# Own rows of a shared expert added by GpSimd in SBUF, and a last sum added by VectorE to TensorE's banks row tile by row tile

## What is computed

```python
def moe_ffn(x2d, ...):                      # x2d: 512 tokens x 1024
    ...                                     # 8 of 64 experts for each token, weights w
    # for each expert: its tokens gathered, swiglu(x[tok], w_exp_gu[e], w_exp_down[e]) * weight,
    # added to the tokens' rows: routed
    return routed + swiglu(x2d, w_sh_gu, w_sh_down)      # the shared expert sees every token

ff = moe_ffn(x, ...)
x = layer_norm_2(DEEPNORM_ALPHA * x + ff, ln3_g, ln3_b)   # DEEPNORM_ALPHA = 2 ** 0.25
```

## Time and profile before

| | |
|---|---|
| median of 3 runs | 2682.42 us (2681.78 to 2683.23) |
| the profiled execution | 2681.46 us, span 2679.5 us |
| TensorE (PE) busy | 2603.9 us, 97% |
| VectorE (DVE) busy | 1963.6 us, 73% |
| ScalarE (ACT) busy | 1410.6 us, 53% |
| GpSimd (POOL) busy | 278.8 us, 10% |
| moved by DMA | 435.49 MB, mean 163 GB/s |

### The profile page before, as it was taken

How to read it: one execution, slowest core, us unless ns; L and a number is a source line. 1 busy time by engine, 2 the same in 40 slices (tenths; PEclk the granted TensorE clock), 3 DMA queues, 4 the chain that set the end, 5 groups by cost and what they waited for, 6 DMA issues and landing times.

```text
span 2679.5 us, 34993 instructions
## 1 busy us (share of the span) xinstructions
PE 2603.9 (97%) x12355; PEld 2031.6 (76%) x12355; DVE 1963.6 (73%) x2844; ACT 1410.6 (53%) x2164; POOL 278.8 (10%) x242
## 2 busy tenths in 40 slices
PE   9999999999999999999999998999999999999996
PEld 7877878788887877888887775587667777777773
DVE  4788765777736985877736738456488999999996
ACT  4766652222324545322333233444456899898893
POOL 0000000000000000000000800000016622222210
PEclk9999999999999999999999999999999999999998
DMA  3222232222323123223233542323139999999997
GB/s 113 71 64 70 63 102 94 95 94 94 97 87 103 46 64 59 81 104 104 67 108 111 151 143 25 110 95 106 57 124 353 396 393 392 401 401 393 393 395 284
DMA packets 260215, 435.49 MB, mean 163 GB/s; under 512 B 45374, under 2 KB 199047, under 8 KB 235267
## 3 DMA queue, kind: packets, MB, share of 16 engines
q1 hardware_dynamic: 241795, 397.71, 42.0%
q0 software_dynamic: 18304, 36.26, 4.4%
HBM read 416.44 MB, written 42.62 MB: 171 GB/s over the span
## 4 chain that ended last, share of the span: by engine, by line
PE 85%; DVE 6%; DMA 3%; ACT 3%; issue 2%; DVEq 0%; SPq 0%; ACTq 0%; POOLq 0%
PE tp L1374 40%; PE tp L2081 4%; PE tp L2083 4%; PE tp L2082 4%; PE tp L1330 2%; PE tp L1480 2%; PE tp L1482 2%; PE tp L1481 2%; PE mp L2103 2%; PE mp L2105 2%; PE mp L2104 2%; PE tp L1421 2%; PE tp L2069 2%; PE tp L1879 1%; DMA uT<-in_w_exp_gu 1%
## 5 line engine op out<-in xcount | busy, mean ns | idle before, releaser
L1374 PE MATMUL tp<-sq_r,arena_r 128*128 128x512 f32 x1056 | 413.8, 392 | 5.8 <-DVE uT_r L2982 3.5
L1374 PE MATMUL tp<-uT_r,arena_r 128*128 128x512 f32 x1056 | 411.7, 390 | 0.0
L1374 PE MATMUL tp<-sq_r,wring_r 128*128 128x512 f32 x1056 | 411.7, 390 | 0.0
L1374 PEld LDWEIGHTS tp<-sq_r,arena_r 128*128 128x128 f32 x1056 | 198.6, 188 | 50.8 <-issue 7.3
L1374 PEld LDWEIGHTS tp<-sq_r,wring_r 128*128 128x128 f32 x1056 | 198.7, 188 | 41.7
L1374 PEld LDWEIGHTS tp<-uT_r,arena_r 128*128 128x128 f32 x1056 | 198.6, 188 | 41.3 <-issue 0.5
L2954 DVE TENSOR_TENSOR wring_r<-wring,arena_r 128x2048 fp32r<-128x2048 f32 x82 | 187.2, 2322 | 48.8 <-ACT arena_r L2244 48.5
L1374 PE MATMUL tp<-arena_r,wring_r 128*128 128x512 f32 x564 | 219.4, 389 | 0.0
L2492 ACT ACTIVATE arena<-arena 128x512 f32<-128x512 f32 x44 | 27.8, 633 | 288.1 <-DVE arena L3040 288.0
L2244 ACT ACTIVATE arena_r<-wring 128x2048 fp32r<-128x2048 f32 x82 | 152.2, 1902 | 39.4 <-DVE arena L3144 11.8
L3895 DVE TENSOR_TENSOR arena_r<-arena,arena_r 128x1024 fp32r<-128x1024 f32 x128 | 150.2, 1213 | 0.5 <-ACT arena_r L2839 0.5
(11 more groups left out here) (633 smaller groups left out, 6261.2 us busy)
## 6 DMA issues: line engine op xcount, KB each, us to landing
wring<-in_w_exp_gu SPq DMA_DIRECT2D x64, 1024.0 KB
arena<-in_w_exp_down SPq DMA_DIRECT2D x64, 1024.0 KB
uT<-in_w_exp_gu SPq DMA_DIRECT2D x32, 1024.0 KB
sq<-in_w_exp_gu SPq DMA_DIRECT2D x32, 1024.0 KB
wring<-in_f_up_w SPq DMA_DIRECT2D x22, 1024.0 KB, 5.0
wring<-in_f_up_w SPq DMA_DIRECT2D x44, 512.0 KB, 6.4
wring<-in_f_down_w SPq DMA_DIRECT2D x32, 448.0 KB, 5.3
wring<-in_a_in_proj SPq DMA_DIRECT2D x42, 256.0 KB, 2.7
```

Of the source, the lines that this page charges most:

```text
L1374: ins = nc.tensor.matmul(b[:], parts[wp][:, kk, m * P:(m + 1) * P], xparts[xp][:, kk, :], start=n_k == 0 and q == 0, stop=n_k == k - 1 and ...
```

## The change

The tokens' own rows leave TensorE. ScalarE now takes the banks of the shared expert alone, without a factor; GpSimd adds the own rows to each taken tile in SBUF (`own_row`, eight additions of 128x512), and signals `pool_tables`. The buffers are swapped: row tiles 0 and 1 go to `raw`, row tiles 2 and 3 to `ye`, and because `ye` is where the own rows of tiles 0 and 1 lie, ScalarE waits for two and then four additions before the fifth and the seventh tile. It waits for all eight before it rounds the first down weights. SyncE stores a row tile when its additions are done. GpSimd does four additions ahead of the gather of expert 2 and four ahead of that of expert 3. The index products and the one-hot tables move forward, the transposes of expert 1 go into the middle of expert 0's products, and VectorE's low parts are reordered. ALPHA comes in at the end, in VectorE's first addition.

At the end TensorE adds the tables 2, 5, 6 and 7 and no longer VectorE's sum. VectorE adds the tables 0, 1, 3 and 4, and when TensorE's banks of a row tile are complete it adds them to its own sum (`add_total`), one row tile ahead of the norm. ScalarE's sum of the rows now reads `fin` in SBUF and waits for `sums_ready`.

```diff
-        rest_halves = [[y[:, 512 * half:512 * half + 512] for half in range(2)] for y in ye]
-        rest_halves += [[raw[2 * k + half][:, PAD:PAD + 512] for half in range(2)] for k in range(2)]
+        rest_halves = [[raw[2 * k + half][:, PAD:PAD + 512] for half in range(2)] for k in range(2)]
+        rest_halves += [[y[:, 512 * half:512 * half + 512] for half in range(2)] for y in ye]
...
-                sp.wait_ge(tile_evac, RES_TILES - 8 + 2 * c + 2)
+                sp.wait_ge(pool_tables, 4 + 1 + 2 * c + 2)
                 rows = rest[c * P:(c + 1) * P, :]
-                if c < 2:
-                    sp.dma_start(rows, ye[c]).then_inc(first_ranks, 16)
+                if c >= 2:
+                    sp.dma_start(rows, ye[c - 2]).then_inc(first_ranks, 16)
                 else:
                     for half in range(2):
                         sp.dma_start(rows[:, 512 * half:512 * half + 512], rest_halves[c][half]).then_inc(first_ranks, 16)
...
+            def own_row(i):
+                pool.wait_ge(tile_evac, RES_TILES - 8 + i + 1)
+                natural = rest_halves[i // 2][i % 2].rearrange("p (q k) -> p q k", k=NK)
+                by_feature = row_tok[i // 2].rearrange("p (k q) -> p q k", k=NK)
+                G.tensor_tensor(natural, natural, by_feature[:, 64 * (i % 2):64 * (i % 2) + 64, :], ALU.add).then_inc(pool_tables, 1)
+
             put_entries(range(0, 6))
             m_gather(0, 0, 0, 1)
-            put_entries(range(6, 8))
+            put_entries(range(6, 7))
             m_gather(1, 1, 1, 2)
-            put_entries(range(8, 9))
+            for i in range(4):
+                own_row(i)
             m_gather(2, 0, 2, 3)
+            for i in range(4, 8):
+                own_row(i)
             m_gather(3, 1, 3, 4)
-            put_entries(range(9, 14))
...
-            def m_gu(n, b, q):
+            def m_gu(n, b, q, halfway=None):
                 wait(moe["xlo"], n + 1)
                 wait(moe["act"], n - 1)
                 hi, lo = [w[:, :].rearrange("p (k n) -> p k n", n=512) for w in (wgu_hi[b], wgu_lo[q])]
                 out = gu_bank(n, b)[0:CAP, :]
                 for k in range(NK):
+                    if k == 4 and halfway:
+                        halfway()
...
-            def own_row(i):
-                pe.wait_ge(tile_evac, RES_TILES - 8 + i - NBANK + 1)
-                by_feature = row_tok[i // 2].rearrange("p (k q) -> p q k", k=NK)
-                nc.tensor.matmul(down_bank(i), ident[:], by_feature[:, 64 * (i % 2):64 * (i % 2) + 64, :], start=True, stop=False)
-
...
-                nc.tensor.matmul(down_bank(i), sact_hi[k][:, rows], shd_hi[:, k, half], start=False, stop=False)
...
-            for i in range(NBANK):
-                own_row(i)
+            def first_half(i):
+                pe.wait_ge(tile_evac, RES_TILES - 8 + i - NBANK + 1)
+                shared_down(i, 0)
+
             pe.wait_ge(rt["weights"], 4 + NK + 4)
             for i in range(NBANK):
-                shared_down(i, 0)
-                if i in (0, 3):
-                    m_idx(i // 3, i // 3, i // 3)
+                first_half(i)
+                if i == 2:
+                    m_idx(0, 0, 0)
             pe.wait_ge(rt["weights"], 4 + NK + 5)
             for i in range(8):
                 if i >= NBANK:
-                    own_row(i)
-                    shared_down(i, 0)
+                    first_half(i)
                 shared_down(i, 1).then_inc(tile_done, 1)
                 tiles.inc()
-                if i in (1, 3):
-                    m_idx(2 + i // 2, 2 + i // 2, i // 2)
+                if i in (0, 2, 4):
+                    m_idx(1 + i // 2, 1 + i // 2, (1 + i // 2) % 2)
                 if i == 6:
                     m_turn(0, 0, 16)
             assert tiles.s == RES_TILES
-            m_turn(1, 1, 16)
-            m_gu(0, 0, 0)
+            m_gu(0, 0, 0, halfway=lambda: m_turn(1, 1, 16))
...
-
-            def add_sum(c):
-                pe.wait_ge(sums_ready, c + 1)
-                add_rank(c, rest_rows)
-
-            def add_last(c):
+            for c in range(TC):
+                pe.wait_ge(late_ranks[c], 16 * 2)
+                add_rank(c, rank_rows[5])
+            for c in range(TC):
                 pe.wait_ge(row_in[c], 16 * 3)
                 add_rank(c, rank_rows[6])
                 add_rank(c, rank_rows[7], last=True).then_inc(rank_sums, 1)
-
-            add_sum(0)
-            for c in range(1, TC):
-                add_sum(c)
-                add_last(c - 1)
-            add_last(TC - 1)
...
-            for c in range(TC):
-                for half in range(2):
-                    take(rest_halves[c][half], scale=ALPHA)
-                if c == 2:
-                    m_xhi(0, 0)
+            for i in range(7):
+                if i == 4:
+                    act.wait_ge(pool_tables, 4 + 1 + 2)
+                if i == 6:
+                    act.wait_ge(pool_tables, 4 + 1 + 4)
+                take(rest_halves[i // 2][i % 2])
+            m_xhi(0, 0)
+            take(rest_halves[3][1])
+            m_ghi(1, 1, 1, 32)
             m_xhi(1, 1)
-            m_ghi(1, 1, 1, 32)
             m_silu(0, 0)
+            act.wait_ge(pool_tables, 4 + 1 + 8)
             m_dhi(0, 0, 0, 16)
             m_acthi(0)
...
-                act.wait_ge(rank_sums, c + 1)
+                act.wait_ge(sums_ready, c + 1)
                 for half in range(2):
-                    ins = nc.scalar.activation(summed[half], total[c][half][:], ACT.Identity, accum_out=row_sums[:, c, half:half + 1])
+                    ins = nc.scalar.activation(unread[half], fin[c][:, 512 * half:512 * half + 512], ACT.Identity, accum_out=row_sums[:, c, half:half + 1])
...
+                if j == 1:
+                    m_onehot(0, 0, 0)
                 dve.wait_ge(rt["weights_hi"], 9 + j)
                 V.tensor_tensor(sact_lo[:, j, :], sact[:, j, :], sact_hi[j].bitcast(F32), ALU.subtract).then_inc(rt["weights"], 1)
...
-            m_onehot(0, 0, 0)
             m_onehot(1, 1, 1)
             assert nconv.s == CONVS
             m_conv(0, 0, 0, 0)
@@ -3929,14 +3932,14 @@
             m_onehot(3, 3, 1)
             m_glo(0, 0, 0, (0,))
             m_conv(2, 0, 2, 0)
+            m_onehot(4, 4, 0)
+            m_conv(3, 1, 3, -1)
             m_glo(0, 0, 0, (1,))
-            m_conv(3, 1, 3, -1)
-            m_onehot(4, 4, 0)
-            m_glo(0, 0, 0, (2,))
             m_xlo(0, 0)
-            m_glo(0, 0, 0, (3,))
+            m_glo(0, 0, 0, (2, 3))
+            m_glo(1, 1, 1, (0, 1))
             m_xlo(1, 1)
-            m_glo(1, 1, 1)
+            m_glo(1, 1, 1, (2, 3))
             m_act(0, 0, swt[0])
             m_dlo(0, 0, 0)
             m_actlo(0)
...
-                    add_rows(c, rank_rows[0])
+                    chain.inc()
+                    V.scalar_tensor_tensor(fin[c], fin[c], ALPHA, rank_rows[0][:, c, :], ALU.mult, ALU.add).then_inc(dve_chain, 1)
+                    added[c] = chain.v
...
-            def add_late(c):
+            for c in range(TC):
                 dve.wait_ge(late_ranks[c], 16 * 2)
-                for r in (4, 5):
-                    add_rows(c, rank_rows[r], last=r == 5)
+                add_rows(c, rank_rows[4])
+
+            def add_total(c):
+                dve.wait_ge(rank_sums, c + 1)
+                dve.wait_ge(dve_chain, added[c])
+                for half in range(2):
+                    s = slice(512 * half, 512 * half + 512)
+                    ins = V.tensor_tensor(fin[c][:, s], fin[c][:, s], total[c][half][:], ALU.add)
+                ins.then_inc(sums_ready, 1)
...
+                    ins = V.scalar_tensor_tensor(centred[half], fin[c][:, s], neg_mean[:, c:c + 1], g3[half], ALU.add, ALU.mult)
...
-                    V.scalar_tensor_tensor(fin[c][:, s], fin[c][:, s], inv_std[:, c:c + 1], b3[half], ALU.mult, ALU.add).then_inc(fin_ready, 1)
-
-            for c in range(TC):
-                add_late(c)
+                    V.scalar_tensor_tensor(fin[c][:, s], centred[half], inv_std[:, c:c + 1], b3[half], ALU.mult, ALU.add).then_inc(fin_ready, 1)
+
+            add_total(0)
             for c in range(TC):
                 mean_of(c)
                 link(centred_gain(c))
+                if c + 1 < TC:
+                    add_total(c + 1)
                 scale_of(c)
                 scaled_bias(c)
```

17 lines of the change are left out of this document (9 added, 8 removed).

## The result

| | before | after |
|---|---|---|
| median | 2682.33 us (9 runs, 2679.57 to 2683.23) | 2689.11 us (9 runs, 2685.6 to 2690.4) |
| the profiled execution | 2681.46 us, span 2679.5 | 2687.01 us, span 2685.3 |
| mean granted TensorE clock | 0.993 | 0.989 |

The ratio is 1.0022, 95% interval 1.0013 to 1.0030: a little slower, 6.8 us by the medians and 5.6 by the profiled executions. The forecast of 2682.7 was 6.4 us too low; the range held the time. A loss of this size is by the prediction's own bound of 0.2% just on the slower side. That the range held it is luck: its upper end, 2689.9, stood for additions of 2.2 us, and they took 1.5.

What follows compares the result with a forecast made beforehand. Weight transfers were taken to pace the experts, not TensorE. Start -2.3 us plus end +2.6 us gives +0.3 on 2682.42, so 2682.7 us; range 2675.8 to 2689.9 us.

Steps and rivals of the forecast that it cites:

- the prediction's own bound of 0.2%: Whole kernel: a change within 0.2% (5.4 us) is about what a measurement can't tell from none.
- The price of an addition: GpSimd's own-row additions at the start: 1.3 us each, plus 0.08 between two.
- the rival's reason: Start: strided additions cost nearly double, as on TensorE, delaying expert 3's weights; slower, up to 2689.9 us; chance 0.24.
- GpSimd and VectorE in turns: Start: last four additions alternate with VectorE's low parts through a shared SBUF port; the eighth ends at 2027.0.
- TensorE 4.2 us earlier at expert 0: Start: VectorE finishes expert 0's activation at 2032.1 instead of 2036.28, so TensorE is 4.2 us earlier.
- The six entries moved behind the last gather cost nothing: Start, GpSimd's queue: moved table entries cost nothing, since GpSimd is busy only 44.5 of 60 us.
- The experts' end depends on when the stream of weights begins: Experts: transfers set the pace; expert 3's weights issue at 2027.6 instead of 2029.94, ending the experts 2.3 us earlier.
- The prediction's own sign: Experts: if the forecast is right, ScalarE shows more and earlier waits for weights than before.
- The end: Last norm: 22.3 us instead of 19.7, 2.6 us longer, with a mean every 5.1 us.

Runs made afterwards that it cites:

- run 8: Changed kernel with one entry issued behind each of the eight additions instead of behind gather 3; 2693.06 us, ratio 1.0039.
- run 7: Changed kernel with two of its nine entries behind gather 3 put back ahead of the additions; 2685.09 us, ratio 1.0008.
- Run 11: Changed kernel with entries spread, the old end, and expert 3's weights issued ahead of the last two row tiles' stores; 2682.17 us, ratio 0.9997.
- run 12: Kernel before, with only expert 3's weights issued ahead of the last two row tiles' stores; 2680.66 us, ratio 0.9998.
- run 5: Changed kernel with five entries between gather 3 and gather 4 and two in each of steps 1 to 10; 2683.90 us, ratio 1.0006.
- run 3: Changed kernel with three entries instead of nine between gather 3 and gather 4, the others in later steps; 2684.95 us, ratio 1.0008.
- run 4: Changed kernel with twelve entries instead of nine between gather 3 and gather 4; 2696.24 us, ratio 1.0048.
- run 9: Changed kernel with two entries back ahead of the additions, none in step 0, two in each of steps 1 to 9; 2683.65 us, ratio 1.0006.

## Why the prediction was right or wrong

**The price of an addition: right.** 1.3 us plus 0.08 was forecast, 1.5 measured. That is 1.2 times the 1.27 us by size of an addition without the stride, so the stride may cost something on GpSimd, but not the doubling that was the rival's reason: the additions are not dear.

**GpSimd and VectorE in turns: wrong in form.** The step let VectorE do a low part between two additions. In fact it was held through each group of four (5.79 us for 0.15 us of work). For the additions that was good: they ended at 2025.14, not 2027.0. For VectorE it was dear, and still the transposes of expert 0's activation came only 1.7 us later than forecast (2.5 us earlier than before, from the mark, instead of 4.2). The Trainium skill, "SBUF — State Buffer", section "Who interferes with whom", says the first to issue holds the ports that both share and the other is blocked until it is done. By that rule one addition would have been the price of a wait; the trace shows a wait for four, and for one where an entry stood between (run 8).

**TensorE 4.2 us earlier at expert 0: sign right.** It was 2.5 us from the mark. The prediction took the half clock after pauses to cost up to 2.2 us at expert 1; the first pitch was 11.24 instead of 9.81, 1.4 us. Between the runs without a wait in it, it was anything from 0 to 2.5, the larger ones where TensorE had paused five times instead of three.

**"The six entries moved behind the last gather cost nothing": the step that failed.** The lists show two entries moved behind gather 3, seven becoming nine, not the six of the prediction nor the three of the section on the change. The prediction looked at GpSimd's busy share, 44.5 of 60 us, and not at who waits behind the entries. The queue is in order, and gather 4 stands behind them. Before, seven entries took 11.7 us (2031.40 to 2043.08) and gather 4 followed with 0.3 us between, so each entry more would put it off. By the 1.7 us an entry that these rows give with its pause, nine from 2027.40 would have let gather 4 go at 2042.8, no later than before. But after the change they took 2.3 each. An entry can take as little as 0.98 us. In the traces before and after, between 2000 and 2300 us, all 27 entries of 1.5 us or more overlap a VectorE low part of 128x1024, and of the 33 shorter ones only 4 do. The entry at 2032.99 lasted 3.49 us, until 0.85 us after the pair of low parts begun at 2033.29 was over. That the low parts lengthen the entries is thus read from these overlaps; no run took the low parts away. What the runs show is the place: in the old one the two entries took 1.0 us each (run 7), and moving them back alone brought gather 4 forward by 4.5 us from the mark, expert 11 by 5.5 and the median by 4.0. Count and place were tested both ways: twelve entries +7.1 us, three -4.2, seven -4.0 on the changed kernel's median, and without the additions the wait stays. Run 7 leaves 0.9 of the 6.4 us that the changed kernel loses up to expert 11. That is the cause of the start's loss, shown.

**"The experts' end depends on when the stream of weights begins": wrong, and the second step that failed.** The prediction took the transfers as the pace of the experts and TensorE's gain as given back in waits for weights. But TensorE was idle for 0.5 us of 480.0 in the kernel before: the weights made ScalarE wait, 23.7 us in all, and hardly TensorE. The prediction's own sign, more and earlier waits on ScalarE, came out the other way, 5.6 us and the first at 2548 instead of 2339. Its reading of an idle queue ahead of the weights was narrow as well: 20 GB/s at 2015 stands between 427 GB/s from 2008 to 2012 and 434 from 2022. Expert 3's weights left 4.0 us earlier than before from the mark (28.7 against 32.7), and the experts ended 4.3 us later. Run 11 issued them 5.6 us earlier still and run 12 moved them in the kernel before; in both ScalarE waits up to 1.9 and 2.0 us in the same stretch, and the experts 11 to 63 take 480.1 and 480.5 us, as before. In all runs but run 5 this stretch is 478.0 to 481.8 us, whatever the start of the stream. It grows a little with the sum of ScalarE's waits: 478.0 us at 3.0 us of waits (run 3), 479.1 at 12.0 (run 4), 480.0 at 23.7 (before), 481.8 at 31.4 (run 8). The five kernels that reach expert 11 within 148 us (run 5 left out) take 480.0 to 480.8 from there; of the other eight, five take 478.0 to 479.1 and three 480.0 to 481.8. Why the waits for weights stand where they do remains open. I read 9.34 us for 17 experts as a pace of the transfers; it was a local delay of 2 us.

**The end: right.** +2.6 was forecast, 21.8 - 19.7 = +2.1 measured, a mean every 5.00 us instead of 5.1.

**The sum.** Forecast -2.3 + 2.6 = +0.3. Measured by the same steps: to expert 11 +6.4, to expert 63 -2.0, to the landing -0.3, end +2.1, together +6.1 from the mark (before rounding). That is 5.8 us over the forecast: 6.6 up to expert 63, less 0.3 at the landing and 0.5 at the end. Of the 6.6, run 7 takes back 2.6 by the stretches (4.0 us by the medians): the gather behind nine entries. The rest is in the main the 2.3 us that the earlier stream was to gain and that no run shows, and then the pauses and the halved clock at the start.

**The range.** It held the time, but not by its reasons. Its upper part was for dear additions that delay the weights. The additions were not dear and the weights left early; what made the time was priced at nothing.

## What to carry to other kernels

An instruction moved on an in-order queue costs nothing only if nothing that somebody waits for stands behind it: look at the next gather, not at the engine's busy share. Price it at its new place too, by what VectorE does there: an entry's instruction of 1 us was up to 3.5 us long beside VectorE's low parts. A wait on one engine is no pace of the program: ask how long the engine behind it was idle. And work taken from an engine that sets the pace can come back as pauses, and with them a lower clock: of the 13.8 us removed from TensorE 2.5 were left at expert 0, behind waits of 3.22, 2.83 and 1.26 us and stretches at half the clock.

## What the runs showed of the hardware

GpSimd's additions in direct succession shut VectorE's two-input instructions out for the whole group: 5.79 us for a 128x1 operation that takes 0.15, and 0.75 once an entry stood between two additions. An indirect DMA's instruction on GpSimd took 1.0 to 3.5 us, and every entry of 1.5 us or more between 2000 and 2300 us overlapped a low part of VectorE. The gathers that TensorE waited for in the chains of waits landed 7.9 us (run 9, issued at 2135.55) to 11.3 us (run 8, at 2037.88) after their issue, with the DMA engines busy for 0.9 of the time or more. And the clock after nearly the same pauses is not the same from one execution to the next: in the changed kernel it was 0.71 of full speed from 2032 to 2036 and in run 5 it was 1.00, for first pitches of 11.24 and 9.81 us. A single profile of this start can therefore be off by 1.4 us by itself, more than half of the 2.3 us that was forecast for it.
